# GpSimd's order of work at the start of layer 0, an earlier first load of the modulation's weights, and weight blocks split in halves

## What is computed

```
def _layer(x, cond, pl, lambda_init, rope=None, ctx_kv=None):
    ada = (jax.nn.silu(cond) @ pl['w_ada'] + pl['b_ada']).astype(x.dtype)
    sh1, sc1, g1, sh2, sc2, g2 = jnp.split(ada[:, None, :], 6, axis=-1)
    h = x * (1 + sc1) + sh1
    y, k, v = _token_mixers(h, pl, lambda_init, rope, ctx_kv)   # h @ w_in, three mixers, @ w_out
    x = _layer_norm(DEEPNORM_ALPHA * x + g1 * y, pl['ln1_g'], pl['ln1_b'])
    h = x * (1 + sc2) + sh2
    m = jnp.square(jax.nn.relu(h @ pl['w_mlp1'])) @ pl['w_mlp2']
    x = _layer_norm(DEEPNORM_ALPHA * x + g2 * m, pl['ln2_g'], pl['ln2_b'])
    return x, k, v
```

## Time and profile before

| | before |
|---|---|
| median of 3 runs | 3781.52 us (3779.92 to 3782.53) |
| the profiled execution's own time | 3773.5 us |
| its span | 3771.7 us |
| busy: PE, DVE, POOL, ACT | 3464.9, 1928.8, 1334.9, 1101.1 us |
| mean granted clock of TensorE | 0.966 of full speed |

### The profile page before, as it was taken

The page is one execution under the profiler, slowest core; times in us unless marked ns, Lnnn a source line. Parts: engine busy times, 40 slices in busy tenths (PEclk is TensorE's granted clock), DMA queues, the critical chain, the costliest instruction groups (busy, mean ns, idle before and its releaser), DMA issues. The chain is left out here.

```text
span 3771.7 us, 48305 instructions
## 1 busy us (share of the span) xinstructions
PE 3464.9 (92%) x18386; PEld 2904.5 (77%) x18386; DVE 1928.8 (51%) x2787; ACT 1101.1 (29%) x2020; POOL 1334.9 (35%) x682
## 2 busy tenths in 40 slices
PE   6899997898899999999988999788899999999996
PEld 3676876777788888888867777677777888888885
DVE  3047565875744434434552765387674344344347
ACT  3212154772511111111152113467534111111114
POOL 2336554101533232332364574430125323223232
PEclk8999998999999999999999999899999999999998
DMA  7577647512111111111117764744201111111101
GB/s 254 211 248 223 200 129 201 121 61 81 34 35 46 34 40 40 35 45 34 34 53 257 225 194 159 197 107 121 82 12 45 41 38 39 40 34 44 35 23 56
DMA packets 285272, 368.48 MB, mean 98 GB/s; under 512 B 16888, under 2 KB 203494, under 8 KB 283783
## 3 DMA queue, kind: packets, MB, share of 16 engines
q1 hardware_dynamic: 211586, 212.63, 19.5%
q10 hardware_dynamic: 73476, 152.83, 11.9%
HBM read 275.48 MB, written 81.53 MB: 95 GB/s over the span
## 5 line engine op out<-in xcount | busy, mean ns | idle before, releaser
L768 POOL TENSOR_TENSOR RH<-RAW,ONE 128x1024 fp32r<-128x1024 f32 x200 | 389.0, 1945 | 1534.2 <-PE PS L927 685.3
L927 PE MATMUL PS<-HH,RH 128*128 128x512 f32 (+1 forms) x2744 | 615.6, 368 | 69.7 <-issue 26.3
L772 POOL TENSOR_TENSOR RL<-RAW,RH 128x1024 fp32r<-128x1024 f32 x240 | 579.5, 2416 | 128.0 <-ACT RH L1903 107.0
L927 PEld LDWEIGHTS PS<-HH,RH 128*128 128x128 f32 x2744 | 471.6, 195 | 189.5 <-issue 96.7
L927 PE MATMUL PS<-HL,RH 128*128 128x512 f32 (+1 forms) x2744 | 584.6, 356 | 0.0
L927 PE MATMUL PS<-HH,RL 128*128 128x512 f32 (+1 forms) x2744 | 578.8, 353 | 0.0
L2553 DVE SCALAR_TENSOR_TENSOR XT<-PS,ADA,XT 128x512 f32<-128x512 f32 (+1 forms) x704 | 453.8, 662 | 244.1 <-PE PS L1419 240.6
L927 PEld LDWEIGHTS PS<-HL,RH 128*128 128x128 f32 x2744 | 466.1, 191 | 74.4
L927 PEld LDWEIGHTS PS<-HH,RL 128*128 128x128 f32 x2744 | 460.6, 189 | 70.9
L2078 ACT ACTIVATE RB<-PS 128x512 f32<-128x512 f32 (+1 forms) x192 | 101.1, 526 | 1391.0 <-PE PS L927 1391.0
L2537 DVE TENSOR_TENSOR PS<-PS,RB 128x512 f32<-128x512 f32 (+1 forms) x192 | 117.2, 610 | 746.4 <-ACT RB L2078 746.4
(11 more groups left out here) (264 smaller groups left out, 4505.6 us busy)
## 6 DMA issues: line engine op xcount, KB each, us to landing
RAW<-in_w_mlp_dram SPq DMA_DIRECT2D x128, 512.0 KB, 3.9
ADW<-in_w_ada_dram ACTq DMA_DIRECT2D x80, 512.0 KB, 5.5
RAW<-const_dram SPq DMA_DIRECT2D x52, 512.0 KB, 4.1
RAW<-in_w_in_dram SPq DMA_DIRECT2D x44, 512.0 KB, 4.7
z_scratch<-ZST ACTq DMA_DIRECT2D x40, 256.0 KB, 3.3
x_scratch<-XT SPq DMA_DIRECT2D x4, 2560.0 KB, 12.7
QH<-q_hi SPq DMA_DIRECT2D x32, 320.0 KB, 9.9
QL<-q_lo SPq DMA_DIRECT2D x32, 320.0 KB, 11.0
```

Of the source, the lines that this page charges most:

```text
L768: nc.gpsimd.tensor_tensor(RH[:, s, :], RAW[:, p, :], ONE[:].broadcast_to([128, 1024]), ALU.mult)\
L772: nc.gpsimd.tensor_tensor(RL[:, s, :], RAW[:, p, :], RH[:, s, :].bitcast(F32), ALU.subtract)\
L927: mm = pe.matmul(out, w[:, s, k * 128:(k + 1) * 128], m(k), start=(n == 0 and k == 0), stop=(n == 2 and k == KT - 1))
```

## The change

It has three parts.

1. At the start of layer 0 GpSimd splits blocks 2 and 3 before the low parts of chunk 1, and the low parts of chunk 2 come behind block 5 instead of ahead of it. SP asks for blocks 2 and 3 ahead of the 18 small loads.
2. ScalarE asks for the modulation's round 0 right behind chunk 0's `first_h`, then makes chunk 1's first two feature tiles; the rest of chunk 1 and 2 is spread over four tiles instead of five.
3. Each split works on two halves of 512 columns: high part first half, high part second half, low part first half, low part second half. This adds 200 + 240 = 440 instructions.

```
@@ SyncE, start @@
                 sp.dma_start(filt_d[:, t].rearrange("l p n -> p l n"), FOUT[:, n % 4]).then_inc(fout_stored[n % 4].sem, 16)
+            for n in (2, 3):
+                load_block(0, B_IN + n, column_block(w_in, 0, COLUMNS[n]), True)
             layer_vectors(0)
...
-                    if l or n > 1:
+                    if l or n > 3:
                         load_block(l, B_IN + n, column_block(w_in, l, COLUMNS[n]), True)
@@ GpSimd, split @@
+                first, second = slice(0, 512), slice(512, 1024)
+                own = b if b < B_HIGH else b - HIGHS
                 if B_HIGH <= b < B_OUT:
                     pool.wait_ge(hi_scalar.sem, hi_scalar.at(l, b + 1 - B_HIGH))
                 else:
-                    nc.gpsimd.tensor_tensor(RH[:, s, :], RAW[:, p, :], ONE[:].broadcast_to([128, 1024]), ALU.mult)\
-                      .then_inc(hi_split.sem, 1)
-                    own = b if b < B_HIGH else b - HIGHS
-                    pool.wait_ge(hi_split.sem, hi_split.at(l, own + 1) + i * per_i)
-                nc.gpsimd.tensor_tensor(RL[:, s, :], RAW[:, p, :], RH[:, s, :].bitcast(F32), ALU.subtract)\
+                    for part in (first, second):
+                        nc.gpsimd.tensor_tensor(RH[:, s, part], RAW[:, p, part], ONE[:].broadcast_to([128, 512]), ALU.mult)\
+                          .then_inc(hi_split.sem, 1)
+                    pool.wait_ge(hi_split.sem, hi_split.at(l, 2 * own + 1) + i * (2 * per_i))
+                nc.gpsimd.tensor_tensor(RL[:, s, first], RAW[:, p, first], RH[:, s, first].bitcast(F32), ALU.subtract)
+                if not B_HIGH <= b < B_OUT:
+                    pool.wait_ge(hi_split.sem, hi_split.at(l, 2 * own + 2) + i * (2 * per_i))
+                nc.gpsimd.tensor_tensor(RL[:, s, second], RAW[:, p, second], RH[:, s, second].bitcast(F32), ALU.subtract)\
                   .then_inc(blk_ready.sem, 1)
@@ GpSimd, start of layer 0 @@
-            for n, (q, j0, j1) in enumerate(((1, 0, 3), (1, 3, 6), (1, 6, 8), (2, 0, 8))):
-                low_of_h(q, j0, j1)
-                split(0, B_IN + 2 + n)
+            split(0, B_IN + 2)
+            split(0, B_IN + 3)
+            low_of_h(1, 0, 3)
+            split(0, B_IN + 4)
+            low_of_h(1, 3, 6)
+            split(0, B_IN + 5)
+            low_of_h(1, 6, 8)
+            low_of_h(2, 0, 8)
@@ ScalarE @@
             first_h(0, 0, KT)
+            act.wait_ge(fout_ready.sem, TT)
+            w, c = ADA_BLOCKS[0][0]
+            for p in range(2):
+                act.dma_start(ADW[:, p], w_ada[w].rearrange("(k p) n -> p k n", p=128)
+                              [:, 2 * p:2 * p + 2, 512 * c:512 * c + 512]).then_inc(ada_in.sem, 16)
+            first_h(1, 0, 2)
...
-                        for q, j0, j1 in (((1, 0, 3),), ((1, 3, 6),), ((1, 6, 8),), ((2, 0, 4),), ((2, 4, 8),))[at:at + 1][0] \
-                                if at < 5 else ():
-                            first_h(q, j0, j1)
+                        if at < 4:
+                            first_h(*((1, 2, 5), (1, 5, 8), (2, 0, 4), (2, 4, 8))[at])
...
-                    if at == ada_round_at(l, 0) - 1:
+                    if l and at == ada_round_at(l, 0) - 1:
                         load_ada(0)
```

More of the change, by code:

```diff
@@ L422, in program @@
         raw_in = [signal(f"raw_in{p}", BLOCKS // 2 * 16) for p in range(2)]
-        hi_split = signal("hi_split", BLOCKS - HIGHS)
+        hi_split = signal("hi_split", 2 * (BLOCKS - HIGHS))
         blk_ready = signal("blk_ready", BLOCKS, 1)
```

## The result

| | before | changed kernel |
|---|---|---|
| median (first comparison, 4 runs each) | 3780.72 us | 3748.09 us (3739.05 to 3754.99) |
| ratio to before, 95% interval | | 0.9922 (0.9905 to 0.9939) |
| the same in two later comparisons (6 runs each) | 3774.41, 3776.48 us | 0.9942 (0.9924 to 0.9960), 0.9923 (0.9907 to 0.9940) |
| profiled execution, its own time and span | 3773.5, 3771.7 us | 3754.99, 3753.1 us |

The kernel is faster by 0.6 to 0.8%, 22 to 29 us, where 17.5 us were forecast, and the first median lies 4 us under the range on record. The two profiled executions lie 18.5 us apart, but the changed one was the slowest of its four runs.

What follows compares the result with a forecast made beforehand. PE, busy 92% of the span, was taken as the bound. Terms -10.7 - 5 - 2.5 + 0.7 = -17.5 us took the profiled 3773.5 to 3756.0; with 8.0 added for the median, 3764 us, range 3752 to 3774.

Steps and rivals of the forecast that it cites:

- The start: Start of layer 0: earlier blocks remove PE's waits, round 1's weights are late next; tile 6 at 125.45, -10.7 us.
- The new wait: Start of layer 0, ahead of tile 6: PE waits 10.3 us for round 1's weights, which land at 122.0.
- the slow clock: Start of layer 0: after a long wait PE's matmuls run at the lower clock, costing 2.4 us more.
- Rival C: Start of layer 0: round 1 hardly late, -15.6 to -23.4 us there, -22 to -30 in all; chance 0.10.
- DVE beside the halves: Attention's head 0: DVE's mixes wait less for POOL, 2.5 us a layer back, -5 in all (0 to -9).
- The open question: Attention: no row shows whether DVE gets in between two high halves without a semaphore; no size given.
- Rival B: Attention: halves do not help DVE, so -10 us in all, 3771.5 us; chance 0.15.
- The output projection's tail: DVE's sums beside shorter splits: 1.25 us a layer back, -2.5 in all (0 to -5).
- The chain ahead of attention: SP's last block load waits for two longer low parts without cover: 0.35 us a layer, +0.7 in all.
- The MLP: Its 128 of the 240 blocks: nothing changes, since PE is busy and POOL has idle time.
- D: The split lines' 5% of the chain is real: longer splits cost +9.8 us, 3774 to 3782 us; chance 0.11.
- E: The two MLPs' 128 blocks: halved splits set the pace, +29 us, 3800 us, slower; chance 0.04.

Runs made afterwards that it cites:

- e6: Changed kernel, with ScalarE asking for the modulation's round 1 right behind tile 2's evacuation: 3745.15 us, 0.9908 of the kernel before.
- e8: Changed kernel, with layer 0's two XT stores and the loads behind them asked for behind block 8 instead of 7: 3751.61 us, 0.9924 of before.
- e4_quarters: Changed kernel, with the output projection's blocks split in quarters of 256 columns instead of halves: 3743.48 us, 0.9904 of the kernel before.
- e7: Changed kernel, with round 1 asked for early, XT stored later and the output projection's blocks in quarters: 3741.05 us, 0.9898 of the kernel before.
- e9: Changed kernel, with every split in quarters: 3745.48 us, 0.9904 of the kernel before.

## Why the prediction was wrong in size

**The start** was right in its mechanism and nearly in its size: split length 4.50 us (4.67), block 5 at 102.8 (103.0), XT's store at 103.22 (103.5), ADW asked for at 111.70 (111.5), tile 6 at 124.2 to 124.9 (125.45). The new wait was 11.4 to 14.4 us instead of 10.3; in the profile with 14.42 PE reached it earlier, with tile 5 done at 108.6 and not at 111.7. That tile 6 was met within 1.3 us is in part luck: round 1 landed at 123.0 instead of 122.0, but I had put all 2.4 us of the slow clock ahead of tile 6, and only 0.9 lie there (1.94 us for round 1's matmuls instead of 1.06), the other 1.4 inside it. Behind both, at tile 7, three profiles with the old order have a mean of 141.8 and three of the changed kernel 132.3: -9.6, against -10.7. e6 and e8 show the two causes of the wait one at a time. Rival C did not come; its rule from the Trainium skill (DMA: Bandwidth & Descriptors, Anatomy of one DMA), 4.4 us for the 1 MB, comes nearer where no store stood ahead: from the first issue to the second load's landing it was 5.7 us in e6_round1_early and in e8_x_later, against 11.3 behind the store. The sum has to ask what the queues hold.

**DVE beside the halves was mis-sized, and this is the step that failed**: "So about half of the 4.5 us a layer should come back", -5 in all. The loss was 7.3 and 9.3 us a layer and not 4.5. I had taken it as head 0's stretch less head 1's, as if head 1's were the same work without POOL; the floor of head 0 itself is 31.3 us, not 33.86. The share that halves give back, 60%, was near the half that I took. Ten us by DVE's rows and 12 by PE's instead of five; the upper bound of 9 was drawn from the same row. The open question whether DVE gets in between two POOL instructions without a semaphore is answered by the 3.29 us row: it does. Rival B is refuted by this and by e4_quarters.

**The output projection's tail**: from matmul 4680 to the MLP (4800) 44.8 to 45.2 us with whole splits in three profiles, 43.9 to 44.5 with halves in eight; in layer 1 (13660 to 13740) 33.9 and 32.9. That is -0.8 and -1.0, -1.8 in all, against -2.5. But what DVE loses there was larger than the 3.8 us that I read: quarters take off another 2.2 and 1.5 us, 5.5 us in all.

**The chain ahead of attention**: the forecast of +0.35 a layer is not resolved. PE waits 12.21 us for KK in the changed kernel, and 11.03 and 12.6 in two profiles of before.

**The MLP** and rivals D and E: nothing changed there, with halves or quarters.

**Sum.** -9.6 - 12 - 1.8 = -23, inside the measured 22 to 29 us. It falls in rival C's -22 to -30, but by its number only: C had the gain at the start, where 9.6 came, and not in attention. And the place of the number: I had added 8.0 us, the distance of the profiled execution from the median of 3 runs. Over all series the 39 runs of the kernel before have a median of 3776.5 us and the 16 of the changed kernel 3750.5, so 3781.5 was 5 us high, and the difference is 26 us, near the -23. The comparison in which the number fell out of its range was the most favourable of the three (3780.72 against 3748.09).

What stays open: halves alone measure -20 us (-13 to -26), of which PE's stretches show 14. The rest is no more than the interval allows, and I found no stretch that carries it. Whether e4, e6, e7 and e9 are really faster than the changed kernel isn't settled either: all four intervals overlap with its own.

## What to carry to other kernels

Two engines that exclude each other for a whole instruction are best sized by a run in which one of them is cut down to nothing; a neighbouring stretch that looks alike is no baseline. If such a loss is found, cutting the other engine's instructions into pieces is a way to get it back. It cost POOL, idle nearly two thirds of the time, 0.14 us each here, and that showed only where a chain ran through POOL itself. When a big transfer is due at a fixed place in a queue, each step won ahead of it brings it nearer to somebody's small load: look at what lands behind it, and move both, or the wait only changes its name.

## What was not expected of the hardware

Behind a store of 2 x 2560 KB the DMA engines were full (share 1.00, 410 GB/s). Loads of 512 KB from another queue, issued 8 to 9 us behind it, landed after 10.4 us, where the median of such loads is 5.7 on the changed kernel's page, and a 256 KB store issued 5 us behind it held up ScalarE for 6.13 us. The Trainium skill (SBUF — State Buffer, Who interferes with whom) says that whichever of DVE and GpSimd issues first keeps the shared pair of ports for its whole instruction. The traces agree in both directions: beside high parts of 1.89, 1.05 and 0.61 us the mix took 3.15, 2.29 and 1.87 us, and a pair of high halves took 3.29 us instead of 2.04 when the mix came between them.
